# One stage of a three-block model on one core: the delta rule's solve regrouped and spread over three phases, and the attention beside it taken by pairs of row blocks

## The reference, cut to what matters

```
# RWKV-7 state, 8 heads of 64, per token
sa = einsum('bhvk,bhk->bhv', S, a_t)
S  = S * w_t + sa[..., None] * b_t + v_t[..., None] * k_t
y  = einsum('bhvk,bhk->bhv', S, r_t)
# forgetting attention, 8 heads of 64, query blocks of 128, causal
s = einsum('bhqd,bhkd->bhqk', q_i, k) * scale + c_i - c
o = einsum('bhqk,bhkd->bhqd', softmax(where(mask, s, -inf)), v)
```

## Time and profile before

| | us |
|---|---|
| median of 3 runs | 5164.3 (5156.48 to 5167.5) |
| the profiled execution, whole | 5158.82 |
| its span, first to last instruction | 5156.7 |
| the stage `mix`, first to last PE instruction and on to the next stage's | 3476.2 to 4135.5, which is 659.3 |

### The profile page before, as it was taken

One profiled execution on the slowest core, in us unless ns is written; L12 is line 12 of the kernel. 1 busy time (PEld: TensorE's weight loads), 2 busy tenths in 40 slices (PEclk: granted clock), 3 DMA queues, 4 the chain that ended last, 5 costly groups with the idle time before them and its releaser, 6 DMA issues. The chain is left out here.

```text
span 5156.7 us, 43603 instructions
## 1 busy us (share of the span) xinstructions
PE 4783.8 (93%) x16204; PEld 2450.3 (48%) x16204; DVE 2746.7 (53%) x3858; ACT 1016.3 (20%) x1559; POOL 375.4 (7%) x248
## 2 busy tenths in 40 slices
PE   8999878999999899999978899979999989999998
PEld 3444443444444344444633343428888834344443
DVE  6646654744555522334525654554434356776767
ACT  1003431100000002333221301223343311110111
POOL 0005411000001000002210100000000010000000
PEclk9999999999999999999989999979999989999999
DMA  2221212111112122112122123442211030111111
GB/s 103 83 86 58 86 53 103 66 49 41 45 46 74 62 93 70 58 39 90 54 108 94 57 98 134 159 141 56 52 41 41 17 123 25 41 40 51 39 43 57
DMA packets 192326, 357.81 MB, mean 69 GB/s; under 512 B 103151, under 2 KB 104447, under 8 KB 191864
## 3 DMA queue, kind: packets, MB, share of 16 engines
q1 hardware_dynamic: 176120, 311.40, 18.1%
q0 software_dynamic: 7936, 28.97, 1.6%
q10 hardware_dynamic: 8064, 14.68, 0.7%
HBM read 260.45 MB, written 94.54 MB: 69 GB/s over the span
## 5 line engine op out<-in xcount | busy, mean ns | idle before, releaser
L172 PE MATMUL mlp_bank<-mlp_u,mlp_s 128*128 128x512 f32 x808 | 355.7, 596 | 0.0
L172 PE MATMUL p_bank<-p_t,p_s 128*128 128x512 f32 x672 | 296.5, 598 | 5.6 <-DVEq L1019 5.5
L172 PE MATMUL mlp_bank<-mlp_x,mlp_s 128*128 128x512 f32 x576 | 259.0, 593 | 0.0
L172 PEld LDWEIGHTS mlp_bank<-mlp_u,mlp_s 128*128 128x128 f32 x808 | 155.4, 192 | 196.1 <-issue 192.3
L277 ACT ACTIVATE mlp_p<-mlp_bank 128x512 f32<-128x512 f32 x70 | 41.3, 590 | 937.2 <-PE mlp_bank L172 898.6
L172 PEld LDWEIGHTS p_bank<-p_t,p_s 128*128 128x128 f32 x672 | 128.9, 192 | 168.5 <-issue 165.9
L287 DVE TENSOR_TENSOR mlp_sum_u<-mlp_bank,mlp_p 128x512 f32<-128x512 f32 x70 | 48.4, 692 | 290.0 <-PE mlp_bank L172 275.2
L172 PEld LDWEIGHTS mlp_bank<-mlp_x,mlp_s 128*128 128x128 f32 x576 | 109.8, 191 | 137.4 <-issue 132.1
L172 PE MATMUL mlp_bank<-tail_y,mlp_s 128*128 128x512 f32 x336 | 151.1, 593 | 0.0
L277 ACT ACTIVATE p_p<-p_bank 128x512 f32<-128x512 f32 x30 | 17.9, 597 | 671.7 <-PE p_bank L172 638.5
L732 ACT ACTIVATE mlp_cv<-mlp_raw,mlp_taps 128x1024 f32<-128x1024 f32 x44 | 54.6, 1240 | 437.7 <-DVEq L747 437.7
(11 more groups left out here) (785 smaller groups left out, 9455.1 us busy)
## 6 DMA issues: line engine op xcount, KB each, us to landing
mlp_w<-in_w_up SPq DMA_DIRECT2D x38, 512.0 KB, 3.7
proj<-p_ev SPq DMA_DIRECT2D x38, 512.0 KB, 3.1
first_w<-in_w_in SPq DMA_DIRECT2D x24, 512.0 KB, 4.1
hgnx_merge_g<-proj SPq DMA_DIRECT2D x8, 1536.0 KB, 7.6
tail_mlp_w<-in_w_up SPq DMA_DIRECT2D x22, 512.0 KB
p_w<-in_w_out SPq DMA_DIRECT2D x16, 512.0 KB, 4.3
mid_mlp_w<-in_w_up SPq DMA_DIRECT2D x16, 512.0 KB
mid_mlp_w<-in_w_down SPq DMA_DIRECT2D x16, 512.0 KB
```

What stands on the lines that cost most here:

```text
L172: mm = nc.tensor.matmul(self.bank[product - 1][:, :], lhs[:, p, :], rhs(name, p), start=p == 0, stop=p == kp - 1)
```

## The change

- **The solve.** The chunk's inverse T is no longer formed and multiplied by the two right sides. `z` is the right side itself (`at` times the state, plus `mak` times `vn`, 8 products); `w` applies the block inverse `p4` to it (4); `x1`, `x2`, `sa` each multiply by `h` and add `w` (4 each, the add on DVE: the nilpotent sum of three terms); `s` and `y` are as before. Gone are `an`, `ht`, `q4`, `h2`, `h3`, `tt`, `wt`, `ut` and the old `sa`; `mrk` and the `mak` half of `m_mak` become one job `mak_mrk`, and `m` is 64 columns wide.
- **Three phases.** `RWKV_OPEN` of chunk c+2, `RWKV_BLOCKS` of chunk c+1 and `RWKV_CHAIN` of chunk c are taken one job of each in turn, in place of two chunks step by step.
- **Attention by pairs.** Row blocks 2j and 2j+1 make pair p = 4h+j. The turns of a pair stand among the `scores`, `exp` and `weigh` of the next pair, and `out` after them: `Pr` has four buffers and `PT` is twice as long, `O` has two halves. `turn` brings the two row blocks' blocks next to each other, so that `out` streams 256 columns for each value block but three. `exp` is a job of its own. There are 32 `out` jobs with 32 copies instead of 64, and 80 turns instead of 96.
- **Weaving** is by weights (`weight`), and the list begins with 6 attention jobs. The last out stands at the end.
- **Loads.** `load_open` (7 transfers: `BT`, the halves of `at` and `bt`, `AR`) and `load_blocks` (8 halves) replace the 16; four buffers `AT` are zeroed (15 memsets in place of 13); q and k are loaded before the values, and the value turns wait for the constants.

```diff
-RWKV_STEPS = (("m_mak", "n_mrb"), ("n2", "m2"), ("mrk", "an", "p2", "n4", "m4"), ("vn", "bhn", "p3", "m8"),
-              ("khn", "p4"), ("h", "ht", "q4"), ("h2",), ("h3",), ("tt",), ("wt", "ut"), ("sa", "s", "y"))
+RWKV_OPEN = ("m", "n_mrb", "n2", "m2", "p2", "n4", "m4")
+RWKV_BLOCKS = ("mak_mrk", "p3", "m8", "vn", "p4", "bhn", "h", "khn")
+RWKV_CHAIN = ("z", "w", "x1", "x2", "sa", "s", "y")
+def rwkv_jobs():
+    jobs = []
+    for step in range(-2, NCK):
+        for n in range(len(RWKV_BLOCKS)):
+            for names, c in ((RWKV_CHAIN, step), (RWKV_BLOCKS, step + 1), (RWKV_OPEN, step + 2)):
+                if n < len(names) and 0 <= c < NCK:
+                    jobs.append((names[n], c))
...
+            now = [(kind, h, 2 * j + a) for a in range(2) for kind in ("scores", "exp", "weigh")]
+            order = [now[0], turns[0], now[1], turns[1], now[2], now[3], turns[2], now[4], turns[3], now[5]]
...
-                        product(job, (b["wt"], state[s]), (b["ut"], b["vn"]))
+                    elif name == "z":
+                        need("mak_mrk", "vn")
...
+                        product(job, (at, state[s]), (b["mak"], b["vn"]))
+                    elif name == "w":
+                        need("z")
+                        product(job, (b["p4"], SOLVE["z"]))
+                    elif name == "x1":
+                        need("h", "w")
+                        product(job, (b["h"], SOLVE["w"]))
+                    elif name == "x2":
+                        need("x1")
+                        product(job, (b["h"], SOLVE["x1"]))
+                    elif name == "sa":
+                        need("x2")
+                        product(job, (b["h"], SOLVE["x2"]))
...
-                        for t in range(i + 1):
-                            mm = nc.tensor.matmul(O[e, 0:P], V[h // 2 % 2][:, t, e], PT[:, t, :], start=t == 0, stop=t == i)
+                            for t in range(2 * j):
+                                part(t, both, 2 * t, start=t == 0)
+                            part(2 * j + 1, second, 4 * j + 2)
+                            mm = part(2 * j, both, 4 * j, stop=True)
...
+                    elif name in ("x1", "x2", "sa"):
+                        dve.wait_ge(kept["w"], c + 1)
+                        dve.wait_ge(made[name], c + 1)
+                        nc.vector.tensor_tensor(SOLVE[name][:, :, :], of(job)[:, :, :], SOLVE["w"][:, :, :], ALU.add)\
+                          .then_inc(kept[name], 1)
```

More of the change, by code:

```diff
@@ new lines, with fox_jobs @@
+RWKV_CHAIN = ("z", "w", "x1", "x2", "sa", "s", "y")
+RW_NAMES = RWKV_OPEN + RWKV_BLOCKS + RWKV_CHAIN
+RW_FLIPS = {"vn": "v", "bhn": "bh", "khn": "kh"}
+def rwkv_jobs():
[5 more added lines that the diff above has]
+                    jobs.append((names[n], c))
+    return jobs
+def fox_jobs():
+    jobs = []
+    for p in range(4 * FH + 1):
+        h, j = divmod(p, 4)
+        old = divmod(p - 1, 4)
+        turns = [("turn", *old, u) for u in range(old[1] + 1)] if p else []
+        turns += [None] * (4 - len(turns))
+        if p < 4 * FH:
+            if j == 0 and h % 2 == 0:
+                jobs += [("values", h // 2, b) for b in range(2)]
+            now = [(kind, h, 2 * j + a) for a in range(2) for kind in ("scores", "exp", "weigh")]
+            order = [now[0], turns[0], now[1], turns[1], now[2], now[3], turns[2], now[4], turns[3], now[5]]
+        else:
+            order = turns
+        jobs += [job for job in order if job is not None]
+        if p:
+            jobs.append(("out", *old))
@@ L3477, in fox_jobs, with weight @@
     return jobs
 def mix_jobs():
-    a, b = [job for g in range(8) for job in rwkv_jobs(g)], [job for h in range(8) for job in fox_jobs(h)]
-    FIRST = 14
+    def weight(job):
+        kind = job[0]
+        if kind == "scores":
+            return 2 * (job[2] + 2)
+        if kind == "out":
+            return 2 + 6 * job[2]
+        if kind in ("exp", "weigh"):
+            return 0
+        if kind in ("turn", "values") or kind in RW_FLIPS:
+            return 5
+        return {"z": 16, "s": 16, "y": 24}.get(kind, 8)
@@ L3484, in mix_jobs @@
+    a, b = rwkv_jobs(), fox_jobs()
+    FIRST = 6
     jobs, taken = b[:FIRST], FIRST
-    for n, job in enumerate(a):
+    total, share = sum(weight(job) for job in a), sum(weight(job) for job in b[FIRST:])
+    done = passed = 0
+    for job in a:
         jobs.append(job)
[L3487 to L3490, removed]
+        done += weight(job)
+        while taken < len(b) and (passed + weight(b[taken]) / 2) * total <= done * share:
+            passed += weight(b[taken])
+            jobs.append(b[taken])
+            taken += 1
@@ L3493, in rwkv_and_fox @@
+    return jobs + b[taken:]
 def rwkv_and_fox(nc, src, q, k, v, masks_in, wide_in, causal_in, ident, Y):
     NP = RH // 2
-    RW_NAMES = [name for step in RWKV_STEPS for name in step]
-    MASKED = ("md", "nd", "mo", "mak")
     jobs = mix_jobs()
@@ L3633, in rwkv @@
                     s = c % 2
-                    b, l, ar = BD[s], {n: LB[n][s] for n in still}, AR[c % 4]
+                    b, l, at, ar = BD[s], {n: LB[n][s] for n in still}, AT[c % 4], AR[c % 4]
                     def need(*names):
@@ L3661, in rwkv @@
                     elif name == "n4":
-                        need("m2", "n2")
+                        need("n2")
                         product(job, (b["m2"], b["n2"]))
                     elif name == "m4":
-                        need("m2", "n2")
                         product(job, (b["n2"], b["m2"]))
+                    elif name == "mak_mrk":
+                        pe.wait_ge(blocks_in[s], 16 * 8 * (c // 2 + 1))
+                        product(job, (l["kt"], ar))
                     elif name == "p3":
@@ L3676, in rwkv @@
                     elif name == "h":
-                        need("p4", "m_mak")
+                        need("p4", "m")
                         product(job, (b["mo"], b["p4"]))
[L3679 to L3698, removed]
+                    elif name == "z":
+                        need("mak_mrk", "vn")
                         if c:
@@ L3702, in rwkv @@
                             pe.wait_ge(zeroed, 1)
-                        product(job, (b["wt"], state[s]), (b["ut"], b["vn"]))
+                        product(job, (at, state[s]), (b["mak"], b["vn"]))
[11 more added lines that the diff above has]
+                        product(job, (b["h"], SOLVE["x2"]))
                     elif name == "s":
                         need("sa", "bhn", "khn")
-                        product(job, (b["bhn"], b["sa"]), (b["khn"], b["vn"]))
+                        product(job, (b["bhn"], SOLVE["sa"]), (b["khn"], b["vn"]))
                     elif name == "y":
[L3708 to L3712, removed]
+                        need("n_mrb")
+                        product(job, (state[s], ar[:, :, 1, :]), (SOLVE["sa"], MRB[c % 4]), (b["vn"], MRK[s]))
                     else:
-                        flip(job, l[{"an": "at", "vn": "v", "bhn": "bh", "khn": "kh"}[name]])
+                        flip(job, l[RW_FLIPS[name]])
                 def fox_job(job):
                     kind = job[0]
+                    if kind in ("exp", "weigh"):
+                        return
                     if kind == "values":
@@ L3740, in fox_job @@
                           .then_inc(scored, 1)
[L3741 to L3746 removed]
+                        return
+                    j = job[2]
+                    p = 4 * h + j
@@ new lines, in fox_job @@
+                    if kind == "turn":
+                        u = job[3]
+                        pe.wait_ge(weighed, 2 * p + 2)
+                        pe.wait_ge(turn_kept, turn_no[job])
+                        pairs = [(2 * u, 0), (2 * u, 1), (2 * u + 1, 0), (2 * u + 1, 1)]
+                        if u == j:
+                            pairs.remove((2 * u + 1, 0))
+                        for n, (t, a) in enumerate(pairs):
+                            mm = nc.tensor.transpose(TP[:, n, :], Pr[(2 * p + a) % 4][:, t * P:(t + 1) * P], ident[:, :])
@@ L3814, in _ @@
                 ch = Chain(dve, own)
+                for s in range(4):
+                    nc.vector.memset(AT[s][:, :, :], 0.0)
                 for s in range(2):
```

246 lines of the change are left out of this document (117 added, 129 removed).

## The result

The changed kernel takes 5065.41 us (median of 4, 5063.14 to 5066.24) against 5160.39 (4 runs, 5154.83 to 5167.5); ratio 0.9818, 95% interval 0.9805 to 0.9831. It is 95 us or 1.8% faster. The forecast was 5084, with 5064 to 5126 as its range: the direction holds and the gain is a fifth larger than the sum's. The time stands 1.4 us inside the lower edge of the range, and in the band under 5066 that had a chance of 0.08; the likeliest band began at 5066.

A forecast was written before the change was run, and what follows sets the result against it. The prediction took PE (TensorE) to set the stage's pace, with 84 us lost to waits and the start. It summed 43 + 5.5 + 38 - 8 + 0 = 78.5 us less, forecasting 5084 us, range 5064 to 5126.

The forecast's parts named there:

- band under 5066: Whole kernel: more gained than counted, a time under 5066 us; chance 0.08.
- likeliest band: Whole kernel: attention's waits mostly gone and few new ones, 5066 to 5099 us; chance 0.62.
- Solve, counted: Chunk solve on PE: 384 fewer records at 0.112 us each, 43 us less; bounds 41 and 43.
- Attention, counted: Attention's out on PE: same columns, 32 fewer jobs at 0.17 us; 5.5 us less, bounds 2 loss and 6.5 gain.
- Attention's waits: PE's waits for attention's weigh, copies and banks: 38 of 43 us go by deferring turns and out; bounds 25 and 43.
- New waits, the chain: PE waiting on the serial links z to s: 8 us of new waits; bounds 0 and 56.
- 1 link in 7: Chain links: with DVE busy half the time, one in seven waits 0.5 us, giving the 8 us.
- Start: Stage's opening: earlier RWKV products against later values' turns, costed at nothing; bounds 6 us gain and 12 loss.
- links do not wait (first): Rival on the solve's chain: its links wait, about 40 us less, 5124, band 5099 to 5130; chance 0.22.
- all waits gone: Rival: the 19 us of unnamed gaps go too and the start gains; 97 us less, 5067; no separate chance given.
- wide records are not cheap: Rival on out: 256-column records cost hardly more than 128; 30 us less, 5054; 0.03, in the case under 5066.
- the chain is not near its edge: Rival, slower: the state's chain sets a chunk's pace; at 1.0 us a link 26 us slower, 5190; chance 0.04.

The follow-up runs named there:

- run with doubled adds: The changed kernel with DVE's adds of x1, x2 and sa done twice, 48 more DVE operations: 5075.76 us, ratio 0.9835.
- weaving by number: The changed kernel with its job lists woven by the number of jobs, as in the kernel before, instead of by weights: 5054.65 us, ratio 0.9798.
- run with turns at once: The changed kernel with a pair's turns and out directly behind the pair's own weighs, not among the next pair's scores: 5136.98 us, ratio 0.9954.

## Why the prediction was right, and where its sum was off

By its own steps. The stage went from 663.2 to 567.7, 95.5 us less, where 78.5 were forecast.

- *Solve, counted, 43*: right, the 4208 records are there, and 42.8 us came when as many were put back.
- *Attention, counted, 5.5*: the column price is confirmed (0.107 at 256 columns; no change with 128). The 0.17 of a job was not tested by itself.
- *Attention's waits, 38 of 43*: right in kind, slightly high. 7.9 us on 13 waits stayed (turns for `TP`, `scores`, `out`), 10 with 0.17 each, so 33 went. I named exp and `scores` as late next; the larger rest was the single `TP`, which I did not see in the list, though two turns in a row on one tile can be read there.
- *New waits, the chain, 8*: mis-sized. On `solve_...` 1.7 us and 0.9 of `issue` before the chain's `s` at 4031.39, 5 waits, 3.5 with 0.17 each, all in the last chunk, for which the prediction had 2.5; the middle has none. "1 link in 7" was a guess from DVE's load; the gaps of 1.35 us and more, counted in the same paragraph, cover every link in the middle, as the run with doubled adds shows.
- *The solve's own waits before were left out of the sum*: the step that fails most. I read 3.7 us on the banks and called 19 us small gaps without a name. The view has more, beside the three rows:

```profile
PE mix_bank L3622 <- issue: 3.7, 4, 1.2
PE mix_bank L3622 <- DMA mix_vb<-rw_v: 2.5, 1, 2.5
...
PE mix_s L3738 <- issue: 1.3, 1, 1.3
PE mix_bank L3622 <- DVE mix_bd_p L3832: 1.0, 2, 0.8
PE mix_tp L3723 <- ACT mix_v L3787: 0.8, 1, 0.8
PE mix_bank L3622 <- DVE mix_mrb L3847: 0.7, 1, 0.7
```

  All of PE's waits between the first turn and the end are 49.5 us in 57 waits, 9.1 of them on `mix_bank` and no transfer, plus the load's 2.53. After, they are 13.2 in 22. 36.3 and 35 x 0.17 = 6.0 make **42.3**, where I had a net 38 - 8 = 30: 33 of attention, some 13 of the others, less 3.5 for the new chain.
- *Start, 0*: right in size, because two effects cancel. The values' turns start 4.6 us later (3.7 by the wait, 0.9 as the stage began later), so near 3 to 4 us are lost, as written. But RWKV's products start 7 us earlier and full clock comes 11 us earlier: 0.72 to 0.80 over 43.8 us, 0.08 x 43.8 = 3.5 us gained.
- *The clock in the middle, not in the sum*: the prediction has full clock from 3520 on. The kernel before has one fall there, which the long window of the earlier trace rows rounds away (0.98 from 4000 to 4100, shown in the last section); the changed kernel's trace has none. That is some 2 us.

Together 43 + 5.5 + 42.3 + 3.5 - 3.7 = 90.6, and with the 2 of the clock 92.6 of 95.5 in the stage. The last 3 us no row names. So the mechanism of the prediction holds, but the measured time lies in its range by 1.4 us only, since the terms that were missed (the solve's own waits, the chain, the clock) mostly point one way. The rivals are settled: links do not wait (first), *all waits gone* gave 5067 and is nearest to the measured 5065 though 13 us of waits remain, wide records are not cheap, and the chain is not near its edge.

## What to carry to other kernels

Where one engine sets the pace, price its records by the spacing of their starts and add to each listed wait what the modelled end of the record before it hides (0.17 us here); then a stage is work, waits and clock, and every one of these runs could be read to a few us. A serial chain is cheap if each link stands apart in the list by more than its evacuation takes (here 0.96 us against 1.35 and more), and dear if not (58.7 us for 16 chunks). A list woven by weights should be looked over for neighbours on one buffer: jobs that weigh nothing on one engine still separate others, and the simple weaving by number was 9 us better.

## What the runs showed of the hardware

The granted clock fell in the midst of dense work that was broken by short waits. In the run with turns at once no wait of PE after the first transfer's was longer than 2.8 us, and the granted clock was below 1.00 in four of the eight windows of 50 us between 3600 and 4000, and again (0.97) from 4055 to 4110:

```profile
3600.00:3650.00 50.00, 44.92 (x348) 39.83 (x346) 21.52 (x44) 15.79 (x32) 0.00 (x0) 1.00 0.18 42
3650.00:3700.00 50.00, 45.62 (x305) 39.93 (x306) 20.02 (x39) 14.02 (x27) 0.00 (x0) 0.90 0.11 25
3700.00:3750.00 50.00, 44.26 (x334) 39.59 (x332) 18.72 (x42) 15.25 (x32) 0.00 (x0) 0.97 0.18 46
3750.00:3800.00 50.00, 44.84 (x317) 39.59 (x318) 17.48 (x32) 16.75 (x32) 0.00 (x0) 0.93 0.17 40
3800.00:3850.00 50.00, 45.77 (x348) 41.25 (x347) 23.70 (x51) 16.54 (x35) 0.00 (x0) 0.97 0.19 44
```

(1.00 less the clock) times the length, summed to 4110, is 13 us of the 16 that its waits left open. At 3655.16 eight records took 0.9 us and at 3670.77, behind a wait of 1.25 us, they took 1.7. The kernel before has one such fall:

```profile
4000.00:4100.00 100.00, 92.12 (x730) 84.26 (x729) 38.79 (x83) 39.91 (x83) 0.00 (x0) 0.98 0.10 22
```

Eight records take 1.7 us there from 4044.14, behind a wait of 2.01 us. Most waits of this length, in both kernels, were not followed by a fall, so no run here says which wait brings one. In the run with doubled adds the same came at the bare end of the chain, right behind waits of 1.23 and 1.34 us:

```profile
4035.00:4055.00 20.00, 16.74 (x70) 13.70 (x69) 3.71 (x6) 0.87 (x2) 0.00 (x0) 0.57 0.00 1
```

```profile
4034.18 1.13 PE L3654 MATMUL mix_bank<-mix_solve_x,mix_bd_h 128*128 128x128 f32 x8 [1.23 <-DVE mix_solve_x L3911]
...
4036.98 2.04 PE L3654 MATMUL mix_bank<-mix_solve_x,mix_bd_h 128*128 128x128 f32 x8 [1.34 <-DVE mix_solve_x L3911]
```

The eight records of the second row are given 2.04 us in place of 1.13, the level of 1.2 GHz. From there to the next stage's first record it is 19.3 us, where the changed kernel takes 11.6 (4029.36 to 4040.98); 0.7 of the difference is a longer wait, and 7 us are the clock, more than the three waits of the last chunk together (4.2). So a wait can cost more than its length, and a removed one can give back more.
